# Decode scores as products of 512 columns, probabilities turned on VectorE, old state added through the identity

## What is computed

```python
# 1. decode attention of a sample over its 32 cached pages of 128 tokens (4096 tokens)
scores = q_abs @ ckv.T + q_pe @ kpe.T          # 256 + 64 features, 4 heads, scaled
p      = softmax(scores)                       # the sample's own token is added at the end
o      = p @ ckv                               # 4 x 256 per sample

# 2. RWKV-7 over the prompt, in 16 chunks of 64 tokens, 4 heads of 64 x 64
Z = A_k V + A S_i ;  U = -T Z                   # T: inverse of a unit triangular matrix,
H = K^T V + B^T U (+ S_i) ; S_{i+1} = e * (...)  #    built in 5 doubling levels (X, Y)
O = V A_k' + U A_b + S r
```

## Time and profile before

| | us |
|---|---|
| median of 3 runs | 2016.49 (2016.43 to 2016.64) |
| profiled execution | 2014.29 |
| its span, first to last instruction | 2012.6 |
| around the span in that execution | 1.7 |
| PE busy | 1864.4 (93%) |
| DVE busy | 896.8 (45%) |
| ACT busy | 497.4 (25%) |
| mean granted TensorE clock | 0.967 |

### The profile page before, as it was taken

One profiled execution on the slowest core, in us unless ns is written; L12 is line 12 of the kernel. 1 busy time (PEld: TensorE's weight loads), 2 busy tenths in 40 slices (PEclk: granted clock), 3 DMA queues, 4 the chain that ended last, 5 costly groups with the idle time before them and its releaser, 6 DMA issues. The chain is left out here.

```text
span 2012.6 us, 45810 instructions
## 1 busy us (share of the span) xinstructions
PE 1864.4 (93%) x19360; PEld 1165.3 (58%) x19360; DVE 896.8 (45%) x1984; ACT 497.4 (25%) x1164; POOL 172.1 (9%) x158
## 2 busy tenths in 40 slices
PE   4899999999988999999859999999999888999998
PEld 2565676666655666654326656756566556666543
DVE  2124133332675777653230340332318666776542
ACT  3111012222412343411131110222224123333201
POOL 0010000001333000000000200000212340000000
PEclk9999999999989999979989999999999899999799
DMA  9600001000204766341076001010001056662411
GB/s 383 219 11 27 21 21 32 21 16 16 62 27 137 206 189 188 109 180 42 35 302 216 0 27 32 11 32 22 21 22 50 27 164 197 186 193 88 180 42 43
DMA packets 103927, 191.18 MB, mean 95 GB/s; under 512 B 17162, under 2 KB 87260, under 8 KB 100004
## 3 DMA queue, kind: packets, MB, share of 16 engines
q1 hardware_dynamic: 103716, 188.19, 28.4%
HBM read 175.41 MB, written 21.19 MB: 98 GB/s over the span
## 5 line engine op out<-in xcount | busy, mean ns | idle before, releaser
L774 PE MATMUL PB<-RB,R 128*128 128x344 f32 x1632 | 496.4, 457 | 0.0
L774 PEld LDWEIGHTS PB<-RB,R 128*128 128x128 f32 x1632 | 303.9, 191 | 159.8 <-issue 19.9
L1964 PE MATMUL PB<-RB,R 128*128 128x512 f32 x512 | 221.2, 592 | 0.0
L1598 PE MATMUL PB<-WUQ,Q 32*32 32x256 f32 x5120 | 200.2, 387 | 21.5 <-DVE WUQ L1759 12.9
L1759 DVE STREAM_TRANSPOSE WUQ<-RB 128x512 f32<-128x512 f32 x316 | 203.2, 680 | 18.5 <-DMA RB<-in_cache 15.6
L1964 PEld LDWEIGHTS PB<-RB,R 128*128 128x128 f32 x512 | 97.0, 190 | 120.8 <-issue 118.6
L934 ACT ACTIVATE R<-PB 128x344 f32<-128x344 f32 x90 | 41.2, 458 | 421.9 <-PE PB L774 421.9
L1187 DVE TENSOR_TENSOR PB<-PB,CST 128x128 f32<-128x128 f32 x64 | 18.8, 294 | 226.3 <-PE PB L794 226.3
L1598 PEld LDWEIGHTS PB<-WUQ,Q 32*32 32x32 f32 x5120 | 90.1, 105 | 47.7 <-issue 30.5
L622 PE MATMUL PB<-RB,R 128*128 128x344 f32 x288 | 87.5, 467 | 10.8 <-PEq L225 10.8
L622 PEld LDWEIGHTS PB<-RB,R 128*128 128x128 f32 x288 | 56.6, 197 | 40.9 <-issue 14.0
(11 more groups left out here) (355 smaller groups left out, 2629.8 us busy)
## 6 DMA issues: line engine op xcount, KB each, us to landing
RB<-in_cache SPq DMA_DIRECT2D x512, 160.0 KB, 2.6
R<-in_w_ada SPq DMA_DIRECT2D x16, 1536.0 KB, 16.9
R<-in_w_in SPq DMA_DIRECT2D x44, 512.0 KB, 3.7
RB<-in_w_out SPq DMA_DIRECT2D x8, 1024.0 KB, 10.2
RB<-out_x_stream SPq DMA_DIRECT2D x2, 4096.0 KB
out_x_stream<-RB SPq DMA_DIRECT2D x16, 512.0 KB
RB<-in_x_prompt SPq DMA_DIRECT2D x1, 4096.0 KB
RB<-in_w_kv SPq DMA_DIRECT2D x2, 1280.0 KB, 5.7
```

The lines of the kernel that those rows point to most:

```text
L774: mm = pe.matmul(jobbank(j)[:, 0:CH], ring[:, blkno[n] % 4, k, :], hT[:, k, chunk(c)], start=(k == 0), stop=(k == KT - 1))
L1598: mm = pe.matmul(PB[qp[o], 2 * (h % 2) + q % 2, 0:256], Q4[qp[q], g, :], k[qp[q], c], start=(g == 0), stop=(g == NB - 1), skip_group_check ...
L1964: mm = pe.matmul(PB[0:n, 2 * (t % 2) + hf, :], mixT[:, k, cols(t)], wo[:, k, hf * 512:(hf + 1) * 512], start=(k == 0), stop=(k == 5))
```

## The change

Four things change, all in the decode stage.

1. S becomes 4 products of 512 columns, one for each row group q, on the diagonal tiles (q, q), all four into bank h % 2. The scores of a half lie in one bank.
2. Since the scores now lie with tokens of one row group in one partition quarter, a 32 x 32 block transpose suffices: PT on TensorE and its four ACT copies go, and one DVE transpose of 128 x 512 (`TP`) writes `PT` directly. EX writes `prb` in order. MX reduces one bank, then combines four quarters instead of two halves: six small operations after the reduction, instead of four.
3. H takes the old state in through the identity on TensorE (4 more products of 64 columns for each H). `Sg`, G and the DVE step of H go; two ACT copies with the decay as scale write the new state.
4. AK has bank 2 to itself, TA bank 3 and TB bank 4; their waits on other users of banks 4 and 6 go. Z waits for `ak_done` and for `oo_done` of the pair before. The three lists are written anew.

```diff
-            sc_ = lambda h: PB[:, 2 * (h % 2):2 * (h % 2) + 2, 0:256]
+            sc_ = lambda h: PB[:, h % 2, :]
-            chain = ("Z", "U", "H", "G", "O")
+            chain = ("Z", "U", "H", "O")
             PE_PAIR = (
-                "S00 S01 Z0 MA U0 PT- S02 H0 S03 S04 PV- X1 S05 Y1 S06 S07 Z1 S08 S09 U1 X2 S10 H1 Y2 S11 PT0 S12 OO "
-                "X3 PV0 Y3 S13 S14 S15 X4 AK TA Y4 S16 S17 TB S18 X5 S19 Y5"
+                "AK S00 MA S01 S02 Z0 PV- U0 X1 S03 S04 Y1 H0 S05 TB S06 S07 X2 S08 S09 Y2 Z1 S10 S11 X3 U1 TA Y3 S12 "
+                "H1 S13 X4 S14 S15 S16 Y4 PV0 S17 X5 S18 S19 OO Y5"
             DVE_PAIR = (
-                "T02 T03 T04 MA T05 T06 H0 LV T07 T08 T09 Y1 T10 MX0 T11 G0 T12 D H1 Y2 T13 T14 T15 G1 T16 Y3 T17 T18 "
-                "T19 AK Y4 T20 T21 MX1"
+                "T02 T03 TP- MA T04 T05 T06 LV T07 Y1 T08 T09 T10 T11 T12 Y2 T13 T14 MX0 Y3 T15 T16 TP0 T17 T18 T19 "
+                "Y4 T20 T21 AK MX1"
             ACT_PAIR = (
-                "Z0 U0 PT- MA X1 Z1 U1 X2 EX0 PT0 OO X3 X4 TA X5 TB Y5 EX1"
+                "Z0 MA X1 U0 TB X2 H0 Z1 X3 U1 EX0 H1 X4 X5 TA Y5 EX1 OO"
...
# PE, H: the old state through the identity
+                                for w in range(2):
+                                    pe.matmul(B[hp[w], f, :], i64[hp[w]], S0[hp[w], i % 4, f, :], start=False, stop=False, skip_group_check=True)
...
# PE, S
-                            k = KTr[:, (NB * h + g) % 4].rearrange("p (s c) t -> p c s t", c=2)
-                            for c in range(2):
-                                for q in (0, 2, 1, 3):
-                                    o = 2 * (q // 2) + c
-                                    mm = pe.matmul(PB[qp[o], 2 * (h % 2) + q % 2, 0:256], Q4[qp[q], g, :], k[qp[q], c], start=(g == 0), stop=(g == NB - 1),
-                                                   skip_group_check=True, tile_position=(32 * q, 32 * o))
+                            k = KTr[:, (NB * h + g) % 4].rearrange("p s t -> p (s t)")
+                            for q in range(4):
+                                mm = pe.matmul(sc_(h)[qp[q]], Q4[qp[q], g, :], k[qp[q]], start=(g == 0), stop=(g == NB - 1),
+                                               skip_group_check=True, tile_position=(32 * q, 32 * q))
-                        elif what == "PT":
...
# ACT, H
+                            for f in range(2):
+                                op = act.activation(S0[:, (i + 1) % 4, f, :], PB[:, 6, f * 64:(f + 1) * 64], ACT.Identity, scale=ecol[:, f, i:i + 1])
...
# DVE, MX and TP
-                            dve.tensor_reduce(mxa, sc_(h), AX.XY, ALU.max)
-                            dve.drain()
-                            dve.tensor_copy(mxb[0:64], mxa[64:128])
-                            dve.tensor_copy(mxb[64:128], mxa[0:64])
-                            dve.drain()
-                            dve.tensor_tensor(mx16[:, h:h + 1], mxa, mxb, ALU.max)
+                            dve.tensor_reduce(mxa, sc_(h), AX.X, ALU.max)
+                            dve.drain()
+                            dve.tensor_tensor(mxb[0:64], mxa[0:64], mxa[64:128], ALU.max)
+                            dve.drain()
+                            dve.tensor_tensor(mx16[0:32, h:h + 1], mxb[0:32], mxb[32:64], ALU.max)
+                            dve.drain()
+                            for q in range(1, 4):
+                                dve.tensor_copy(mx16[32 * q:32 * q + 32, h:h + 1], mx16[0:32, h:h + 1])
...
+                            dve.transpose(PT.rearrange("p s m -> p (s m)"), prb).then_inc(pp_done, 1)
```

More of the change, by code:

```diff
@@ L1377, in bass_hybrid_trunk @@
             Tm, Tc, XX, Lo = (RB[:, o:o + P].rearrange("p (d c) -> p d c", d=4) for o in (16088, 16216, 16344, 16472))
-            Zs, Sg = (RB[:, o:o + P].rearrange("p (f v) -> p f v", f=2) for o in (16600, 16728))
+            Zs = RB[:, 16600:16728].rearrange("p (f v) -> p f v", f=2)
             Bc = RB[:, 19456:19584].rearrange("p (d c) -> p d c", d=4)
@@ L1425, in pair_plan @@
                             out.append((2 * p + int(w[1]), w[0], int(w[2])))
-                        elif w[:2] in ("PT", "PV", "MX", "EX"):
+                        elif w[:2] in ("TP", "PV", "MX", "EX"):
                             out.append((2 * p - 1 if w[2] == "-" else 2 * p + int(w[2]), w[:2], 0))
@@ L1479, in prepare @@
                             if p >= 1:
-                                pe.wait_ge(oo_done, p)
+                                pe.wait_ge(ak_done, p)
                             for d, c, f, w in heads:
-                                mm = pe.matmul(B6[hp[w], d], pT[hp[w], 2 + f, at1(c)], A13[hp[w], bass.ds(0, 2, step=2), f, at(c)],
+                                mm = pe.matmul(B2[hp[w], d], pT[hp[w], 2 + f, at1(c)], A13[hp[w], bass.ds(0, 2, step=2), f, at(c)],
                                                start=True, stop=True, skip_group_check=True)
@@ L1541, in follow @@
                         if n[0] == "Z":
+                            pe.wait_ge(ak_done, p + 1)
                             pe.wait_ge(ta_done, p + 1)
                             pe.wait_ge(tb_done, p + 1)
+                            if p >= 1:
+                                pe.wait_ge(oo_done, p)
                             pe.wait_ge(st_done, i + 1)
@@ L1699, in _ @@
                             if h:
-                                act.wait_ge(pp_full, h)
-                            act.activation(prb.rearrange("p (s q c) -> p q s c", s=8, q=2), sc_(h).rearrange("p q (s c) -> p q s c", s=8),
+                                act.wait_ge(pp_done, h)
+                            act.activation(prb, sc_(h),
                                            ACT.Exp, bias=nmb, scale=SCALE, accum_out=L16[:, h:h + 1]).then_inc(xe_done, 1)
-                        elif what == "PT":
-                            act.wait_ge(pp_full, h + 1)
-                            if h:
-                                act.wait_ge(pg_free, 2 * h)
-                            t4 = PB[:, 4, :].rearrange("p (s w m) -> p s w m", s=4, w=2)
-                            for w in range(2):
-                                for e in range(2):
-                                    op = act.activation(PT[hp[w], :, e * 64:(e + 1) * 64], t4[hp[e], :, w, :], ACT.Identity)
-                            op.then_inc(pp_done, 1)
                         elif what == "FC" and g == 3:
@@ L1797, in prepare @@
                             dve.transpose(Tc.rearrange("p d c -> p (d c)"), Tm.rearrange("p d c -> p (d c)")).then_inc(tm_done, 1)
-                    def follow(p, n):
-                        B = PB[:, 6, 0:P].rearrange("p (f v) -> p f v", f=2)
-                        if n[0] == "H":
-                            i = 2 * p + int(n[1])
-                            dve.wait_ge(hh_full, i + 1)
-                            for f in range(2):
-                                op = dve.scalar_tensor_tensor(S0[:, (i + 1) % 4, f, :], B[:, f, :], ecol[:, f, i:i + 1], Sg[:, f, :], ALU.mult, ALU.add)
-                            op.then_inc(st_done, 1)
-                        elif n[0] == "G":
-                            i = 2 * p + int(n[1])
-                            if i + 1 < NCH:
-                                if p == NS - 1:
-                                    dve.drain()
-                                dve.tensor_tensor(Sg, S0[:, (i + 1) % 4], ecol[:, :, i + 1:i + 2].broadcast_to([P, 2, 64]), ALU.mult)
-                                if p == NS - 1:
-                                    dve.drain()
                     for h, what, g in pair_plan(DVE_PAIR):
-                        if what == "rw" and g[0] in chain:
-                            if h >= 1:
-                                follow(h - 1, g)
-                        elif what == "rw":
+                        if what == "rw" and g[0] not in chain:
                             prepare(h, g)
```

47 lines of the change are left out of this document (23 added, 24 removed).

## The result

The changed kernel takes 2073.32 us (median of 4 runs, 2072.11 to 2075.43), the kernel before 2016.57 us (2016.43 to 2016.76) beside it: ratio **1.0282, 95% interval 1.0265 to 1.0300**, so slower by 57 us. The forecast was 2106.5 us and its range 2080 to 2134 us. The sign is right, the time lies 7 us under the range, and the growth is 57 us where 90 were forecast. So the two profiles differ by 61 us.

The account below looks back on a forecast made before the run. TensorE with its fixed order was taken to set the decode pace: +7.0 us a pair, +56 us a layer over eight pairs, less savings at start and end, taken as +45 a layer, +90 in all: 2106.5 us, range 2080 to 2134.

Parts of the forecast that it names:

- Tiles: Score steps in decode: half the instructions on half the tiles, 0.864 us instead of 0.432, +8.64 us for each pair.
- small waits: TensorE within a pair: four short waits for transposed buffers, 0.6 to 1.0 us, mostly vanish with longer S, -0.8 us.
- PT, H, shapes: TensorE's other words in a pair: PT gone -1.16 us, more H products +0.5, one tile-shape change fewer -0.2.
- Issue of instructions: TensorE in S: the number of instructions sets no bound, since eight start inside the first 0.05 us of a step.
- The pair of 27.76 us as undisturbed, and -1 us a layer for waits named issue: Decode stage: 27.76 us taken as an undisturbed pair; issue waits of 2.9 us on S in layer 1 shrink, -1 us.
- Page waits and clock at the start of the stage: Start of decode, each layer: pages land before a slower TensorE needs them, -5.8 us; clock then holds, -2 us.
- The end: End of decode, each layer: less TensorE idling before PT and PV, -2.5 us, and a clock falling less, -0.8 us.
- VectorE, ScalarE, PV0, banks as free: Rest of a pair: VectorE +0.6 us, fewer ScalarE copies, later PV0 and own banks cost or gain TensorE nothing.
- number 1: Rival, score step: issue or an array-wide limit sets its cost, so S stays 0.43 us; 2000 us, faster; chance 0.06.
- number 2: Rival, score step: four row groups writing one bank take turns, 3.46 us a step; 2940 us; chance 0.02.
- Number 3: Rival, decode stage: fewer active tiles drop the clock to 1.2 GHz, some 27 us more a pair; 2540 us; chance 0.04.
- Number 4: Rival, waits and end: nothing given back, 2144 us; all given back, 2086 us; upper part above 2134 has chance 0.03.

Follow-up runs that it names:

- s512_only: Kernel before with only the new score products (4 of 512 columns on 4 diagonal tiles), old lists, banks and PT kept: ratio 1.0353, pairs 33.6 us.
- before_128cols: Kernel before with each score product of 256 columns cut into two of 128 on the same tile: ratio 1.0619, pairs 36.8 us.
- the second profile: Kernel before, unchanged, profiled again on the chip of the later runs: 2014.4 us, pairs 27.9 us.
- after_8tiles: Changed kernel with eight score products of 256 columns on eight tiles again, AK, TA and TB sharing a bank: ratio 0.9981, pairs 28.2 us.
- the kernels with 128 columns: Kernel before (whole, half or an eighth of page bytes) and changed kernel, score products cut to 128 columns: ratios 1.0619, 1.0473, 1.048 and 1.0601.
- after_256cols: Changed kernel with each score product of 512 columns cut into two of 256 on the same tile: ratio 1.0302, pairs 33.1 us.

## Why the prediction was wrong in size

Step by step, by its own order.

- **Tiles.** Right in the mechanism. Three steps in a row take 0.867 us each for a forecast of 0.864. But over a pair S, with X and Y that lie between on the same tiles, grew by 7.2 us (middle values of the words, 13.9 to 21.1) and not by 8.64, since a word behind S starts on tiles that are already free. Without the small waits the growth was forecast as 8.64 - 1.16 + 0.5 - 0.2 = 7.8 us and measured as 7.2 from the shortest words; with them it was forecast as 7.0 and measured as 6.6.
- **PT, H, shapes.** Near: forecast as -0.86 us a pair together, and the difference of s512_only to the changed kernel is -0.56 us. PT took 1.2 us a pair as forecast. H takes 0.85 us from its start to the next word's where it took 0.61, +0.24 for +0.25 forecast.
- **Issue of instructions "is no bound that could pay this back".** Wrong, and this is the root of the error. Eight instructions in 0.05 us showed how fast instructions start that are already there, not how fast new ones arrive. The Trainium skill (TensorEngine Tiling, Instruction Overhead) gives some 60 cycles for each matmul, 25 ns at 2.4 GHz. It isn't the limit met here: in the trace products on different tiles start 6 to 10 ns apart, and at 25 ns each the 1,182 products of a pair of before_128cols would need 29.6 us (an estimate from the page's figure), where the pair took 36.8. The limit here is the arrival of blocks of 256 instructions, one in 3.9 us.
- **The pair of 27.76 us as undisturbed, and -1 us a layer for waits named issue.** This is the step that failed. The pair of 27.76 us wasn't undisturbed: without stops it takes 26.4 us, and this one has stops of some 0.3 us inside PT0, AK and Y5, all at seams. The mean pair was 28.2 us (27.9 in the second profile). The stops are 1.5 to 1.8 us a pair, 12 to 14 us a layer, and go with the change; for them the sum had only the 1 us a layer for issue, beside 0.8 us a pair for small waits, which were there (26.4 against 25.8). The same trace would have told me: S08 with S09 took from 1.02 to 2.48 us in different pairs, and I explained the 1.28 us of one of them by a buffer. Its extra 0.26 us lie inside S09, behind the step's only wait.
- **Page waits and clock at the start of the stage, -5.8 and -2 us.** Right: TensorE's waits for pages are 0.5 us in layer 0 and none in layer 1, and the clock held 1.00.
- **The end, -3.3 us.** The sum is about right, its two terms less so: from the last Y5 to the work behind the stage 15.9 us instead of 20.0 in layer 0, 17.5 instead of 20.6 in layer 1. Of these 4.1 and 3.1 us, 1.7 and 1.8 lie ahead of PV (2.5 forecast) and 2.4 and 1.3 behind it (0.8 forecast, for the clock). The clock stood at 0.50 from 860 to 875 us in the kernel before and at 1.00 from 890 to 900 us in the changed one, the same part of the end. The wait for PT is gone, and PV starts 0.9 us after the one larger wait left, Z for ScalarE's copy of OO:

```profile
885.78 0.33 PE L1551 MATMUL PB<-R 64*64 64x64 f32 x4 [1.84 <-ACT RB L1688]
886.66 3.28 PE L1612 MATMUL PB<-RB 128*32 128x256 f32 x32
```

- **VectorE, ScalarE, PV0, banks as free.** Right: TensorE is busy for over 99% of the stage. But the same parts won nothing with S on eight tiles (after_8tiles): what they took off the words, the stops took back.
- **Outside the stage** I forecast nothing. The profiled execution of the changed kernel is 2.6 us later at the start of the first stage and 2.8 us later between the stages. That is near the 4.3 us by which the two profiled executions stand off their medians, and was not pursued.

The sum, made again for one layer: words with their small waits +6.6 us and stops -1.6 us (the mean of both profiles) give +5.0 us a pair, +40; page waits -6, clock -2: +32 before the end, for +32.6 and +30.8 measured. With -3.3 for the end, +29 a layer, +57 for both. The forecast had +56, -7.8, -1 and -3.3. Of the 2.0 us a pair between +7.0 and +5.0, the stops make 1.6 and the overlap behind S 0.4.

Of the rivals, number 1 (S stays at 0.43 us) is refuted by the 0.867 us of a step, and number 2 (one bank in turns) too. The Trainium skill (TensorEngine Tiling, Gotcha 1: PSUM Pressure) says that different row tiles can't access one PSUM bank at the same time. Here four row groups write one bank, each its own quarter of the partitions, and a step takes 2 x 0.433 us, the time of one tile's stream alone, so the measurement decides against it for such writes. Number 3 (the clock falls) is refuted: 1.00 and 0.99 in the stage with four tiles of sixteen at work. Number 4 saw the right sign of what was left over, but its lower end of 2086 us was made from the same undersized stops.

**What stays open.** That the stops are late supply rests on four things: they lie where the program waits for nothing, they follow the number of instructions whatever the words are, those inside words stand only where the count of instructions has gone up by a multiple of 256, and each ends 1.0 to 1.6 us after a packet of instructions. Why packets start no closer than 3.3 us apart, and how page traffic stretches this a little, no run shows.

## What to carry to other kernels

Count the tiles that work at once before merging small products: half the instructions on half the tiles cost 0.43 us a step here. Before pricing a change of an engine that seems busy, take the mean and the spread of many repeats of its loop and the shortest time of each word; what lies between is time that a change can give back or a gain that it can't reach. And where an engine runs thousands of short instructions, their number is a second bound beside their work, which counts in blocks of 256 and not only on the mean: cutting one of the two pays only until the other is met.

## What the hardware showed that I had not expected

- TensorE stops for up to 2.5 us in the middle of instructions that wait for nothing, at every 256th instruction (matmul or weight load) at which the next 16 KB packet of them is late. In the kernels with 128 columns one packet came in 3.7 to 3.9 us, one instruction in 14.6 to 15.6 ns. At one in 23 ns (33.0 us for 1,420) and one in 19 ns (after_256cols) there were no stops.
- Loading half as many bytes of pages (GB/s 86 instead of 151 in the stretches of the 128-column kernels) eased this by 1.4 to 2.3 us of 36.8; loading an eighth of them eased it no further.
- Stops make the time irregular, so the spread of a loop is a sign of them: pairs of 26.7 to 31.4 us in the kernel before, of 33.00 to 33.07 in the changed one.
